# Head scales spread by two rounded products inside later gate pieces; masks and tables loaded beside other work

## The reference

```python
p = jax.nn.softmax(sc, axis=-1)
a = p[:, :, 0] - lam * p[:, :, 1]
...
o = o * lax.rsqrt(jnp.mean(jnp.square(o), axis=-1, keepdims=True) + RMS_EPS)
o = o * subln_g.astype(jnp.float32) * (1.0 - lam_init)
```

```python
g = jax.nn.sigmoid(gates.reshape(B, S, N_BRANCH, D))
merged = (g[:, :, 0] * (y_attn @ w_br_attn[l])
          + g[:, :, 1] * (y_conv @ w_br_conv[l])
          + g[:, :, 2] * (y_mem @ w_br_mem[l]))
```

## Time and profile before

| | us |
|---|---|
| median of 3 runs | 3476.27 |
| lowest, highest | 3473.62, 3480.43 |
| the profiled execution's own time | 3479.35 |
| its span in the trace | 3477.7 |
| PE busy | 3003.5 (86%) |
| PE weight loads busy | 2369.6 (68%) |
| DVE busy | 1873.6 (54%) |
| ACT busy | 1136.2 (33%) |
| POOL busy | 318.1 (9%) |

### The profile page before, as it was taken

How to read it: one execution, slowest core, us unless ns; L and a number is a source line. 1 busy time by engine, 2 the same in 40 slices (tenths; PEclk the granted TensorE clock), 3 DMA queues, 4 the chain that set the end, 5 groups by cost and what they waited for, 6 DMA issues and landing times. The chain is left out here.

```text
span 3477.7 us, 34599 instructions
## 1 busy us (share of the span) xinstructions
PE 3003.5 (86%) x13230; PEld 2369.6 (68%) x13230; DVE 1873.6 (54%) x2704; ACT 1136.2 (33%) x1950; POOL 318.1 (9%) x472
## 2 busy tenths in 40 slices
PE   7989979888898799989996599949898899648993
PEld 6768857777676676766874488737676588437882
DVE  5543353351565445654534588744465454447884
ACT  3431140310453112152003377621215200237773
POOL 0110030000441002110000100010121000010001
PEclk9999989898899999988998799969998899879997
DMA  3212202222702222202324599633220222458993
GB/s 117 73 63 95 85 29 68 71 85 87 282 1 68 69 95 73 73 4 73 97 81 175 211 391 403 270 115 97 73 73 4 73 88 82 174 203 317 408 406 126
DMA packets 152426, 467.61 MB, mean 134 GB/s; under 512 B 15790, under 2 KB 30024, under 8 KB 126920
## 3 DMA queue, kind: packets, MB, share of 16 engines
q1 hardware_dynamic: 142904, 431.34, 34.5%
q0 software_dynamic: 9360, 34.08, 2.5%
HBM read 413.49 MB, written 51.90 MB: 134 GB/s over the span
## 5 line engine op out<-in xcount | busy, mean ns | idle before, releaser
L161 DVE CAST weights_r<-weights 128x1024 fp32r<-128x1024 f32 (+4 forms) x248 | 208.1, 839 | 751.0 <-DMA weights<-in_w_in 293.2
L154 PE MATMUL ps<-x_cols_hi_r,weights_r 128*128 128x512 f32 x896 | 362.6, 405 | 38.2 <-DVE weights_r L323 24.1
L155 PE MATMUL ps<-x_cols_lo_r,weights_r 128*128 128x512 f32 x896 | 358.5, 400 | 0.0
L156 PE MATMUL ps<-x_cols_hi_r,weights_r 128*128 128x512 f32 x896 | 358.0, 400 | 0.0
L163 DVE TENSOR_TENSOR weights_r<-weights,weights_r 128x1024 fp32r<-128x1024 f32 (+4 forms) x248 | 351.4, 1417 | 8.5
L154 PEld LDWEIGHTS ps<-x_cols_hi_r,weights_r 128*128 128x128 f32 x896 | 171.3, 191 | 84.8 <-DVE weights_r L323 26.2
L982 POOL TENSOR_SCALAR weights<-weights,weight 128x256 f32<-128x256 f32 (+3 forms) x304 | 152.5, 522 | 714.3 <-DVE weight L876 421.5
L926 ACT ACTIVATE weights<-weights,minus_top 128x256 f32<-128x256 f32 (+3 forms) x304 | 167.0, 551 | 148.8 <-DVE minus_top L839 148.8
L155 PEld LDWEIGHTS ps<-x_cols_lo_r,weights_r 128*128 128x128 f32 x896 | 171.4, 191 | 42.2 <-issue 1.4
L156 PEld LDWEIGHTS ps<-x_cols_hi_r,weights_r 128*128 128x128 f32 x896 | 171.1, 191 | 41.7
L154 PE MATMUL ps<-hawk_xT_hi_r,weights_r 128*128 128x512 f32 x384 | 155.5, 405 | 14.9 <-DVE weights_r L323 12.1
(11 more groups left out here) (488 smaller groups left out, 6840.5 us busy)
## 6 DMA issues: line engine op xcount, KB each, us to landing
weights<-in_w_in SPq DMA_DIRECT2D x60, 1024.0 KB, 5.3
raw_pieces<-in_w_exp_down SPq DMA_DIRECT2D x46, 1024.0 KB, 8.2
raw_pieces<-in_w_exp_up SPq DMA_DIRECT2D x36, 1024.0 KB, 7.4
weights<-in_w_exp_gate SPq DMA_DIRECT2D x34, 1024.0 KB, 6.8
raw_pieces<-in_w_exp_gate SPq DMA_DIRECT2D x32, 1024.0 KB, 7.2
weights<-in_w_exp_up SPq DMA_DIRECT2D x30, 1024.0 KB, 7.3
weights<-in_hawk_w_in SPq DMA_DIRECT2D x27, 1024.0 KB, 5.2
weights<-in_w_exp_down SPq DMA_DIRECT2D x20, 1024.0 KB, 8.2
```

The source lines that it names most:

```text
L154: pe.matmul(out, as_r(left[1]), as_r(right[0]), start=start, stop=False)
L155: pe.matmul(out, as_r(left[0]), as_r(right[1]), start=False, stop=False)
L156: return pe.matmul(out, as_r(left[0]), as_r(right[0]), start=False, stop=stop)
L161: dve.tensor_copy(as_r(hi), lo).then_inc(rounded, 1)
```

## The change

1. Merge. The scales (`inv`, 8 x 512) are split into two rounded halves on DVE, at the end of `invert`, ahead of the split of piece 2. ACT makes a rounded table of ones, `chooser`, between its two early roundings. `norm_spread` takes four heads at a time, two rounded products for each, ahead of column tile j = 2 of a gate piece: heads 0 to 3 in piece 4, heads 4 to 7 in piece 6. `scale_heads` follows on DVE: heads 0 to 3 behind `split_branch(1)`, ahead of the split of piece 5; heads 4 to 7 behind `merge(1)`, ahead of the split of piece 7. PE's branch pieces of steps 1 and 2 wait for 4 and 8 scaled heads.
2. Mask of the differential attention: loaded in the projection, by SP behind the loads of its first weight piece; SP waits for it at the projection's end. Its own stage is gone (in both layers).
3. Tables of the dilated attention: loaded by SP inside `column_attention`; POOL waits for them ahead of its first `build`. Their own stage is gone.

```diff
--- before.py
+++ after.py
@@ -201,7 +201,7 @@
     ps = m.ps
     Chunk = namedtuple("Chunk", "job c per tile low turn wn read")
     plan, tiles, lows, turns, weighted, read = [], 0, 0, 0, 0, 0
-    rider = rider or bag(names=(), dve={}, act={}, act_first=None, pool=None, sync=None)
+    rider = rider or bag(names=(), dve={}, act={}, act_first=None, pool=None, sync=None, landed=None)
 
     def tiles_of(job):
 
@@ -281,6 +281,8 @@
                         s.weights_loaded[slot], 16)
                 if n == 0 and rider.sync:
                     rider.sync(sp, s)
+            if rider.landed:
+                rider.landed(sp, s)
 
         @block.vector
         def _(dve):
@@ -688,7 +690,7 @@
 
 
 def column_attention(nc, m, units, n_sets, lag, n_buf, n_slots, mode, tables=None, finish_by="dve", minus_lam=None,
-                     zero_rows=(), zeros=None):
+                     zero_rows=(), zeros=None, loads=()):
 
 
     ps = m.ps
@@ -746,6 +748,8 @@
 
         @block.sync
         def _(sp):
+            for dst, src in loads:
+                sp.dma_start(dst, src).then_inc(s.table_loaded, 16)
             for rows in zero_rows:
                 sp.dma_start(rows.rearrange("(b p) d -> p b d", p=P),
                              zeros[:, :].unsqueeze(1).broadcast_to([P, MAX_BLOCKS, D])).then_inc(s.cleared, 16)
@@ -983,6 +987,8 @@
                                                      ALU.mult, ALU.mult)
                     ins.then_inc(s.scaled, 1)
 
+            if loads:
+                pool.wait_ge(s.table_loaded, 16 * len(loads))
             if quads:
                 build_quad(0)
             if n_tables:
@@ -1428,13 +1434,6 @@
         dist = spare[:, 0:n_dist]
         rows = spare[:, n_dist:3 * n_dist].rearrange("p (a n) -> p a n", a=2)
         at = (0, 256, 256 + SEQ, 256 + 2 * SEQ)
-        with stage(nc, "loaded") as (block, s):
-            @block.sync
-            def _(sp):
-                for g, name in enumerate(("dist_near", "dist_by4", "dist_by16")):
-                    sp.dma_start(dist[:, at[g]:at[g + 1]], a[name]).then_inc(s.loaded, 16)
-                sp.wait_ge(s.loaded, 48)
-
         def build(pool, h):
             for g in range(DIL_GROUPS):
                 part = slice(at[g], at[g + 1])
@@ -1466,7 +1465,8 @@
                             (value(j), keys[:, 256 * j:256 * j + min(TT - j, 2) * P], j * P, min(TT - j, 2) * P) for j in range(TT)],
                         out=6 + h % 2, first=False, finish=lambda dve, bank, h=h: gated_by(yT)(dve, bank, h)))
         tables = dict(n=DIL_HEADS, build=build, free=lambda h, cnt: cnt.pieces[DIL_GROUPS * (h - 1)])
-        column_attention(nc, m, units, 1, 4, 5, 6, "joined", tables)
+        column_attention(nc, m, units, 1, 4, 5, 6, "joined", tables,
+                         loads=[(dist[:, at[g]:at[g + 1]], a[name]) for g, name in enumerate(("dist_near", "dist_by4", "dist_by16"))])
 
 
 
@@ -1864,38 +1864,30 @@
-def diff_attention(nc, m, a, q, k, v, minus_lam):
+def diff_attention(nc, m, a, q, k, v, minus_lam, mask):
-    with Tensors(nc) as sb:
-        mask = sb("mask", [P, SEQ])
-        with stage(nc, "loaded") as (block, s):
-            @block.sync
-            def _(sp):
-                sp.dma_start(mask[:, :], a["mask_causal"]).then_inc(s.loaded, 16)
-                sp.wait_ge(s.loaded, 16)
...
@@ -1936,13 +1928,15 @@
     with Tensors(nc) as sb, stage(nc, "weights_loaded*2", "first_loaded*2", "early_rounded", "first_split", "rounded", "y_split",
                                   "weights_split", "read", "gated",
                                   "multiplied", "added", "picker_ready", "squared", "summed", "norm_step", "rooted", "spread",
-                                  "normed") as (block, s):
+                                  "normed", "chooser_ready", "inv_rounded", "inv_split") as (block, s):
         sig = sb("sig", [P, 4, SEQ])
         prod = sb("prod", [P, 2, SEQ])
         y_hi = [sb("branch_hi", [P, b.tiles, SEQ]) for b in branches]
         sq = y_hi[2]
         picker = sb("head_picker", [P, DA_HEADS, DA_HEADS])
         inv = sb("inv_rows", [DA_HEADS, SEQ])
+        inv_hi = sb("inv_hi", [DA_HEADS, SEQ])
+        chooser = sb("head_chooser", [DA_HEADS, DA_HEADS, P])
         var, root = prod[0:DA_HEADS, 0, :], prod[0:DA_HEADS, 1, :]
         y_base = [0]
         for b in branches:
@@ -1974,14 +1968,14 @@
                     mm = pe.matmul(m.ps[0:DA_HEADS, 4 * BANK:5 * BANK], picker[:, h, :], sq[:, h, :], start=h == 0, stop=h == DA_HEADS - 1)
                 mm.then_inc(s.summed, 1)
 
-            def norm_spread():
-                pe.wait_ge(s.norm_step, 6)
-                for h in range(DA_HEADS):
+            def norm_spread(heads, q):
+                pe.wait_ge(s.inv_split, 1)
+                pe.wait_ge(s.chooser_ready, 1)
+                for h in heads:
+                    pe.wait_ge(s.multiplied, 4 * (q - 1) + h % 4 + 1)
                     bank = (4 + h % 4) * BANK
-                    if h >= 4:
-                        pe.wait_ge(s.normed, h - 3)
-                    pe.matmul(m.ps[:, bank:bank + BANK], m.ident[0:DA_HEADS, h:h + 1].broadcast_to([DA_HEADS, P]), inv[:, :],
-                              start=True, stop=True).then_inc(s.spread, 1)
+                    pe.matmul(m.ps[:, bank:bank + BANK], as_r(chooser[:, h, :]), as_r(inv[:, :]), start=True, stop=False)
+                    pe.matmul(m.ps[:, bank:bank + BANK], as_r(chooser[:, h, :]), as_r(inv_hi[:, :]), start=False, stop=True).then_inc(s.spread, 1)
 
             for r, (q, gate, k0, last) in enumerate(pieces):
                 n, b = steps[q]
@@ -1996,9 +1990,8 @@
                                 mm.then_inc(s.read, 1)
                     norm_sums()
                     continue
-                if r == 2:
-                    norm_spread()
-                    pe.wait_ge(s.normed, DA_HEADS)
+                if not gate and q in (1, 2):
+                    pe.wait_ge(s.normed, 4 * q)
                 pe.wait_ge(s.weights_split, r)
                 if gate:
                     right_hi, right_lo = xT.hi, xT.lo
@@ -2006,6 +1999,8 @@
                     right_hi, right_lo = y_hi[b], branches[b].y
                     pe.wait_ge(s.y_split, y_base[b] + k0 + 4)
                 for j in range(4):
+                    if gate and (q, k0, j) in ((1, 4, 2), (2, 0, 2)):
+                        norm_spread(range(4 * q - 4, 4 * q), q)
                     if k0 == 0 and q:
                         pe.wait_ge(s.gated if gate else s.multiplied, 4 * (q - 1) + j + 1)
                     bank = (j if gate else 4 + j) * BANK
@@ -2035,6 +2030,8 @@
                 act.activation(sq[:, h, :], norm.y[:, h, :], ACT.Square).then_inc(s.squared, 1)
             act.wait_ge(s.weights_loaded[1], 16)
             round_early(*weight_part(m, 1))
+            act.activation(as_r(chooser[:, :, :]), m.ident[0:DA_HEADS, 0:DA_HEADS].unsqueeze(2).broadcast_to([DA_HEADS, DA_HEADS, P]),
+                           ACT.Copy).then_inc(s.chooser_ready, 1)
             round_early(y_hi[0], branches[0].y)
             act.wait_ge(s.norm_step, 1)
             act.activation(root, var, ACT.Sqrt).then_inc(s.rooted, 1)
@@ -2057,14 +2054,16 @@
                 dve.wait_ge(s.norm_step, 2)
                 refine_rsqrt(dve, s.norm_step, 2, var, inv[:, :], root)
                 dve.tensor_scalar(inv[:, :], inv[:, :], norm.factor, None, ALU.mult).then_inc(s.norm_step, 1)
-
-            def scale_heads():
-                for h in range(DA_HEADS):
+                dve.wait_ge(s.norm_step, 6)
+                split(dve, inv_hi[:, :], inv[:, :], s.inv_rounded, 1, s.inv_split)
+
+            def scale_heads(heads):
+                for h in heads:
                     bank = (4 + h % 4) * BANK
                     dve.wait_ge(s.spread, h + 1)
                     dve.scalar_tensor_tensor(out=norm.y[:, h, :], in0=norm.y[:, h, :], scalar=norm.gain, in1=m.ps[:, bank:bank + BANK],
                                              op0=ALU.mult, op1=ALU.mult).then_inc(s.normed, 1)
-                dve.wait_ge(s.normed, DA_HEADS)
+                dve.wait_ge(s.normed, heads[-1] + 1)
 
             def low_early(at, hi, lo, done):
                 for k in range(4):
@@ -2108,12 +2107,14 @@
                     invert()
                 else:
                     split_weights(r)
-                if r == 2:
-                    scale_heads()
                 if q in (1, 2) and gate and k0 == 4:
                     split_branch(q)
+                    if q == 1:
+                        scale_heads(range(4))
                 if r in merge_after:
                     merge(merge_after[r])
+                    if merge_after[r] == 1:
+                        scale_heads(range(4, DA_HEADS))
             merge(len(steps) - 1)
 
 
@@ -2749,14 +2750,18 @@
                 q = bag(hi=ybT[0], lo=sb1("q_lo", [P, DA_HEADS, SEQ]))
                 k = columns_pair(sb1, "k", DA_HEADS, SEQ)
```

(8 more changed lines are left out.)

40 lines of the change are left out of this document (20 added, 20 removed).

## The result

| | us |
|---|---|
| changed kernel, median of 5 runs (lowest to highest) | 3458.16 (3453.96 to 3465.71) |
| kernel before, beside it, 5 runs | 3480.43 (3473.62 to 3482.62) |
| ratio, 95% interval | 0.9943 (0.9924 to 0.9961) |
| the profiled execution's own time, and its span | 3461.89, 3460.2 |

The changed kernel is faster by 0.4 to 0.8%, that is 14 to 26 us. Forecast were 29.

The account below looks back on a forecast made before the run. PE was taken as the bound (busy 86%), DVE counting only where PE waits. Merges -16.3, masks -10.2 and tables -2.5 gave -29.0: 3450.3 us profiled, 3447 as median; range 3437 to 3460, the forecast's own 3440 to 3455.

Parts of the forecast that it names:

- PEclk 1.00 through pieces 4 and 6: Merge: expected sign that PE keeps its full clock through the two pieces that now hold a spread.
- rival B: Merge: the clock falls at each of the four new spreads, 1.9 us each, +7.6 us, 3455; chance 11%.
- Gaps between pieces 1 and 2: Merge: with the spread moved out, 0.75 us remains between these pieces; gains 9.86 and 11.6 us.
- Clock of piece 2: Merge: without the long gap piece 2 keeps full clock, gaining 1.9 us a merge, 3.8 together.
- Price of the spread products: Pieces 4 and 6: rounded products at 0.23 us each, four heads 1.87 us, costing 7.5 us in all.
- Rival C: Merge: an 8-row rounded product takes 0.61 us instead of 0.23, 12 us more on PE, 3459; chance 7%.
- DVE late at piece 8: Merge: DVE's splits end after PE could start piece 8, a new stall of 0.75 us, 1.5 in both merges.
- Merges: Sum over both merges of gaps, piece 2's clock, spread products and the stall at piece 8: -16.3 us.
- Masks: Two differential attentions: 3.5 us less idle at entry plus 1.6 us of better clock each, -10.2 us together.
- Rival A: Differential attentions keep the full clock throughout, 14.5 us an attention, 26 us more in all, 3421; chance 8%.
- Rivals D and E: D: clock never returns in differential attentions, 3507, 2%. E: load stages cost less than they look, 3457, 3%.
- Tables: Dilated attention: scores run before the tables land and DVE scans sooner, -2.5 us, bounds 1 and 5.3.

Follow-up runs that it names:

- the runs with two heads: Changed kernel with each spread of four heads cut in two, two heads ahead of column tiles 1 and 2: 3454.69 us, 0.9931; later fill runs also used it.
- merge alone: Kernel before with only the new merge_branches, masks and tables loaded as before: 3466.63 us, ratio 0.9966.
- fill alone: Changed kernel plus four unread full-height products behind the scores of each of units 0 to 4 of the differential attentions: 3456.27 us, ratio 0.9912.
- entry fill alone: Changed kernel plus four unread full-height products behind the projection's last product ahead of each differential attention: 3457.12 us, ratio 0.9932.
- full height: Changed kernel with scales and chooser filled up with zeros to 128 rows, same number and place of products: 3456.44 us, ratio 0.9929.
- loads alone: Kernel before with only the mask and table loads moved, old merge kept: 3471.03 us, ratio 0.9982.
- new products at the old place: Changed kernel with the rounded products of all eight heads, and their scalings, back between pieces 1 and 2: 3462.12 us, ratio 0.9946.
- the run with both fills and two products a unit: Changed kernel, spreads two heads at a time, four unread products behind the projection, two behind scores of each of first five units: 3437.99 us, 0.9889.

## Why the prediction was right or wrong

The direction held, and so did the gaps and the idle times; the clock inside the pieces with a spread did not. The gain was 20 us by the ratio and 24 by the stages, where 29 were forecast. The profiled execution was to take 3450.3 us and took 3461.9, about 11.6 more: 6.1 in the merges, 0.8 in the tables, 6.4 in the rest of the span, less 1.8 in the masks. Point by point:

- **PEclk 1.00 through pieces 4 and 6**: this is the step that failed. It was called rival B, with 11% and 7.6 us, and rows 3 and 4 had shown few-row products losing the clock already. Three of four spreads lost it, some 1.54 us each (14.97 instead of 13.43 for the piece), 4.6 in all. "1.87 us of few rows stand between full products" was argued, not read; the runs with two heads show that half as many do no harm. Of the 16 spreads of four heads in the profiles that have them (the changed kernel, merge alone, fill alone, entry fill alone) 10 lost the clock; of the 32 spreads of two heads, none, nor of the 4 at full height. Whether one falls differs from execution to execution, so three of four is this profile's luck; 10 of 16 at 1.54 us are about 1 us a spread.
- **Gaps between pieces 1 and 2**: forecast 0.75 us left in each merge, measured 0.62 and 0.64 idle. Right.
- **Clock of piece 2**: 13.09 us before, now 1613.97 - 1602.67 = 11.3. Right.
- **Price of the spread products**: forecast 4 x 1.87 (7.5), measured 4 x 2.23 = 8.9 us, since a piece with a spread and no fall takes 13.43 us instead of 11.20. The spacing of 0.23 was right; what was left out is about 0.1 us at each of four products where the row count changes. Rival C is refuted.
- **DVE late at piece 8**: forecast 0.75 us a merge, measured 0.3 in the first (pieces 7 and 8 take 11.42 and 11.27 us instead of 11.20) and nothing in the second, where PE itself comes later because the clock fell behind the spread in piece 6. The chain was read rightly: DVE's eight splits and that of piece 8 took 12.0 us, from 1664.11 to 1673.80 + 2.29 = 1676.09. With spreads as cheap as forecast and no fall (full height) PE waits 0.5 us in each merge. That most of it did not show is luck: a loss on PE hid it.
- **Merges**: forecast -16.3, measured -10.2. Length of the pieces, from PE's start of one to its start of the next, in us (all others take 11.20 in both kernels):

| | first merge, before | changed | second merge, before | changed |
|---|---|---|---|---|
| up to piece 0 | 7.03 | 6.96 | 7.07 | 7.10 |
| piece 0 | 21.15 | 21.06 | 19.66 | 20.80 |
| piece 1 and what stands behind it | 21.99 | 12.10 | 23.75 | 12.11 |
| piece 2 | 13.09 | 11.30 | 13.04 | 11.31 |
| piece 4 | 11.20 | 14.97 | 11.20 | 14.97 |
| piece 6 | 11.20 | 13.43 | 11.20 | 15.01 |
| pieces 7 and 8 | 22.40 | 22.69 | 22.40 | 22.40 |

In sum: gaps -21.5, piece 2 -3.5, spreads +8.9, falls +4.6, DVE +0.3, and +1.1 in piece 0 of the second merge, for which the forecast had no term. There the clock is at half for 10.2 us instead of 6.8 behind the attention. Of the six merges behind an attention with the old load one has 10.2, of the 22 with the new load 15; whether the shorter attention brings the longer stretch stays open.

- **Masks**: forecast -10.2, measured -12.0. Idle 3.48 each as forecast, and the load beside the projection cost nothing that can be seen: the projections take 177.2 to 178.4 us in the profiles with the old load and 177.2 to 178.5 in those with the new one and no fill behind them. The clock gave 2.5 us an attention instead of 1.6: half clock for 27.3 instead of 34.1 us. It fell where it was said to, in unit 0 or 1; in two other profiles with the new load (loads alone, new products at the old place) it was at half for 30.7 us in three attentions, so some of the 2.5 us is this profile's. Rival A did not happen by itself, but a full clock is worth about what it said, as the run with both fills and two products a unit shows (11.4 us more an attention, where 12.9 had been worked out). Rivals D and E are refuted: the clock came back in every attention, and the idle time went as forecast.
- **Tables**: forecast -2.5. Among the profiles with a mean clock of 0.93 in this stage the two with the old loads have 79.52 us, the six with the new ones 78.9 to 79.2, mean 79.0: it gave some 0.5 us at the same clock, and 1.3 us between the means of all three old and all eleven new ones (80.4 and 79.2). In the two profiles shown below DVE does start its first scan sooner (7.4 instead of 8.2 us after the projection), but that "its wait of 1.27 us for the last score tile goes too" was no gain. It went from unit 0 and came back in unit 1, where DVE waits 2.29 and 0.98 us for PE instead of 1.34. PE's timelines, the kernel before (repeat) first, then the run with two heads at a time:

```profile
443.65 4.61 PE L764 MATMUL ps<-kT,qT 128*128 128x128 f32 x8 [6.00 <-PEq L89]
449.05 2.43 PE L764 MATMUL ps<-kT,qT 128*128 128x128 f32 x8 [0.79 <-DVE minus_top L839]
```

```profile
437.72 2.40 PE L768 MATMUL ps<-kT,qT 128*128 128x128 f32 x8 [1.47 <-PEq L89]
445.45 4.34 PE L768 MATMUL ps<-kT,qT 128*128 128x128 f32 x8 [5.33 <-DVE minus_top L843]
```

Unit 0's eight products used to pay for the half clock (4.61 us); now they are done at full clock, PE idles 5.33 us for the tables all the same, and unit 1's products pay (4.34 us). PE's idle time is the same in sum (6.00 + 0.79 and 1.47 + 5.33 us); it only stands behind unit 0 now.

- **The base**: the forecast started from 3476.27, the median shown; the same kernel had 3478 to 3480.5 in all later series. These 2 to 4 us are in the level of the forecast, not in its difference.

## What to carry to other kernels

Where a few small products stand between large ones, read the granted clock behind them: with few rows of contraction they can cost nearly as much after they have run as while they run (here 1.5 us beside 2.2), and cutting their run in two or filling the rows up with zeros took that cost away. Of the two the zeros were cheaper: a piece takes 13.04 us with them and 13.84 with the run cut in two. Where an idle time goes away, ask which work stood at the low clock behind it and whether it still will. Where two losses stand on two engines, taking one away uncovers the other (DVE at piece 8). And a stage's first profile is one sample: the dilated attention of one kernel took 82.24 and 79.52 us here, at mean clocks of 0.89 and 0.93, so repeat the profile of before ahead of explaining such a size.

## What the runs showed of the hardware

- PE busy without a gap lost the clock behind 10 of 16 runs of eight 8-row products of 512 columns, and kept it behind 4 of 4 of the same products with 128 rows, 120 of them zeros. The Trainium skill, page "TensorE: Matmul & The Clock Gate", section on the HAM clock gate, has the clock follow how busy PE has been; the trace does not agree for products of few rows.
- PE busy for 37.50 of 37.50 us at half clock did not get the clock back while 64-row scores were mixed with full-height fills; in the second attention the same program kept it at 1.00 to the end of the stage. So a full clock could be held here by work that did not bring it back.
- Changing between 128-row and 8-row products cost about 0.4 us a run, there and back: a piece with eight 8-row products in one run took 13.43 us, in two runs 13.84, with the eight products at 128 rows 13.04 (each without a fall of the clock).
